# Two modulation blocks out of the first FFN1 step and into token mixing, one more moved inside the first FFN2 step

## The reference

```
cond = silu(c)
for l in range(2):
    mod = cond @ w_ada[l] + b_ada[l]              # 1024 x 9216
    sh1, sc1, g1, sh2, sc2, g2, sh3, sc3, g3 = split(mod, 9)
    h = rms_norm(x, norm_ffn1[l]) * (1 + sc1) + sh1
    x = x + 0.5 * g1 * swiglu(h, w_gate1[l], w_up1[l], w_down1[l])   # hidden 2816: FFN1
    h = rms_norm(x, norm_mix[l]) * (1 + sc2) + sh2
    x = x + g2 * token_mixing(h, w_in[l], ..., w_out[l])             # three kinds of attention, 16 heads
    h = rms_norm(x, norm_ffn2[l]) * (1 + sc3) + sh3
    x = x + 0.5 * g3 * swiglu(h, w_gate2[l], w_up2[l], w_down2[l])   # FFN2
```

## Time and profile before

| | |
|---|---|
| median of 3 timed runs | 1188.55 us (1175.79, 1188.55, 1189.0) |
| the profiled execution's own time | 1179.13 us |
| its span, first to last instruction | 1177.4 us |
| PE / PEld / DVE / ACT busy | 96% / 87% / 73% / 45% |
| mean granted clock of TensorE | 0.989 |
| HBM read | 256.56 MB, 219 GB/s over the span |

### The profile page before, as it was taken

One profiled execution on the slowest core, in us unless ns is written; L12 is line 12 of the kernel. 1 busy time (PEld: TensorE's weight loads), 2 busy tenths in 40 slices (PEclk: granted clock), 3 DMA queues, 4 the chain that ended last, 5 costly groups with the idle time before them and its releaser, 6 DMA issues.

```text
span 1177.4 us, 20277 instructions
## 1 busy us (share of the span) xinstructions
PE 1135.6 (96%) x7892; PEld 1024.1 (87%) x7892; DVE 864.5 (73%) x1263; ACT 530.3 (45%) x685; POOL 64.7 (5%) x79
## 2 busy tenths in 40 slices
PE   6899999999999999999998999999999998999998
PEld 3599999989898789999987999998989877999997
DVE  5787788798866877666777877888887588645545
ACT  3334334454566543433463344335456545433432
POOL 2101101100000000000001011000000000000000
PEclk9999999999999999999998999999999999999999
DMA  9898899945511667777747988995842155566451
GB/s 304 273 328 300 298 318 312 334 126 172 179 55 55 215 214 239 227 247 256 264 158 243 333 302 295 308 349 156 257 144 91 55 179 171 189 212 192 164 196 72
DMA packets 160371, 258.41 MB, mean 219 GB/s; under 512 B 8365, under 2 KB 127277, under 8 KB 160319
## 3 DMA queue, kind: packets, MB, share of 16 engines
q1 hardware_dynamic: 140739, 182.25, 46.8%
q0 software_dynamic: 19584, 75.50, 19.1%
HBM read 256.56 MB, written 1.05 MB: 219 GB/s over the span
## 4 chain that ended last, share of the span: by engine, by line
PE 81%; DVE 10%; ACT 3%; DVEq 2%; DMA 2%; issue 2%; SPq 0%; ACTq 0%
PE bank L1246 24%; PE bank L1247 24%; PE bank L1248 24%; DVE wlo L854 3%; DVE room L796 2%; PE bank L1585 2%; PE bank L1504 1%; DVEq L798 1%; ACT whi L458 1%; DMA xs<-in_x_dram 1%; DMA ada<-in_w_ada_dram 1%; PE bank L1489 1%; PE bank L1566 1%; DVE xn L955 1%; ACT hTf L486 1%
## 5 line engine op out<-in xcount | busy, mean ns | idle before, releaser
L1246 PE MATMUL bank<-hhi,whi 128*128 128x256 f32 (+1 forms) x1600 | 455.7, 285 | 0.0
L1248 PE MATMUL bank<-hhi,wlo 128*128 128x256 f32 (+1 forms) x1600 | 453.6, 283 | 0.0
L1247 PE MATMUL bank<-hlo,whi 128*128 128x256 f32 (+1 forms) x1600 | 453.5, 283 | 0.0
L458 ACT ACTIVATE whi<-raw 128x2048 fp32r<-128x2048 f32 (+1 forms) x174 | 321.6, 1851 | 8.7 <-PE bank L1693 5.3
L1246 PEld LDWEIGHTS bank<-hhi,whi 128*128 128x128 f32 (+1 forms) x1600 | 306.8, 192 | 4.0 <-issue 1.8
L1247 PEld LDWEIGHTS bank<-hlo,whi 128*128 128x128 f32 (+1 forms) x1600 | 306.8, 192 | 2.4 <-issue 0.5
L1248 PEld LDWEIGHTS bank<-hhi,wlo 128*128 128x128 f32 (+1 forms) x1600 | 306.7, 192 | 0.0
L854 DVE TENSOR_TENSOR wlo<-raw,whi 128x2048 fp32r<-128x2048 f32 (+2 forms) x130 | 281.7, 2196 | 20.0 <-ACT whi L458 19.4
L796 DVE SCALAR_TENSOR_TENSOR room<-ada,cT,room 128x512 f32 (+3 forms) x266 | 170.1, 639 | 22.0 <-issue 2.6
L510 ACT ACTIVATE eb<-bank 128x512 f32<-128x512 f32 x40 | 23.9, 597 | 343.7 <-PE bank L1248 343.7
L972 DVE TENSOR_TENSOR wlo<-raw,whi 128x1024 fp32r<-128x1024 f32 x44 | 53.9, 1225 | 139.7 <-ACT whi L458 138.7
(11 more groups left out here) (218 smaller groups left out, 1134.0 us busy)
## 6 DMA issues: line engine op xcount, KB each, us to landing
ada<-in_w_ada_dram POOLq DMA_DIRECT2D x68, 1024.0 KB, 6.0
raw<-in_w_gate_dram SPq DMA_DIRECT2D x44, 1024.0 KB, 5.9
raw<-in_w_up_dram SPq DMA_DIRECT2D x44, 1024.0 KB, 7.1
raw<-in_w_down_dram SPq DMA_DIRECT2D x44, 1024.0 KB, 6.1
raw<-in_w_in_dram SPq DMA_DIRECT2D x28, 1024.0 KB, 5.4
raw<-in_w_out_dram SPq DMA_DIRECT2D x8, 512.0 KB, 3.2
raw<-in_w_out_dram SPq DMA_DIRECT2D x4, 1024.0 KB, 5.9
room<-in_w_ada_dram POOLq DMA_DIRECT2D x3, 1024.0 KB, 14.0
```

The source lines that it names most:

```text
L458: last = act.activation(dst, src, ACT.Copy)
L1246: pe.matmul(ps, l_hi, r_hi, start=first, stop=False)
L1247: pe.matmul(ps, l_hi, r_lo, start=False, stop=False)
L1248: return pe.matmul(ps, l_lo, r_hi, start=False, stop=last)
```

## The change

Ten of the FFN1 steps (WF1) weigh two blocks each, and the first step none. Mixing weighs five (MID): two in the first projections as before, one ahead of `logits(l, "A0")`, one after `read_out(l, "C10")` and thus ahead of `logits(l, "A1")`, and one after the last slab of w_out. The first FFN2 step weighs its block from slot 1, between the `split_lo` of slot 0 and that of slot 1 for the next step, where it was at the step's start from slot 0. PE's twelve one-column sums between chunk 1 and chunk 2 of mixing become eight, each ahead of a group of three products of chunk 2 ("ki"); the four others go to the mixing tail, where they replace four matmuls of zeros. DVE's `split_lo` of the first FFN2 gate slab goes from between the two halves of the residual to ahead of the last `weigh_mid`; ACT's `split_hi` of the first FFN2 up slab goes from between the two halves of the boundary to ahead of them. At the start POOL waits for the second slab in slot 1 before its first load of the loop.

```diff
-    MID = ADA_L - 3 * NF
+    WF1 = NF - 1
+    MID = ADA_L - 2 * WF1 - NF
+    OWN = NF - AHEAD
...
+            pool.wait_ge(raw_full[1], 16)
             for l in range(L):
                 rows_l = l * KT
-                with pool.Fori(0, NF) as i:
+                with pool.Fori(0, WF1) as i:
                     for k in range(2):
                         fill(k, ada_turn(l, k, i + 1), bass.ds(rows_l, KT), bass.ds(i * (2 * CW) + (AHEAD + k) * CW, CW))
...
+                for n in range(OWN):
+                    m = ADA_L - OWN + n
+                    if n == 0:
+                        fill(1, ada_turn(l, 1, WF1 + 3), bass.ds(rows_l, KT), slice(m * CW, (m + 1) * CW))
+                    else:
+                        fill(0, ada_turn(l, 0, WF1 + 3 + n), bass.ds(rows_l, KT), slice(m * CW, (m + 1) * CW))
...
@@ ACT, boundary @@
-                    if n == 2 and t == 0:
-
-                        act.wait_ge(out_done, nth(l, len(OUT_CHUNKS) - 1, NSLOT + 2))
-                        split_hi(1, turn(l, U_FFN[1]))
@@ ACT, after the output product @@
-                act.wait_ge(out_done, nth(l, len(OUT_CHUNKS) - 1, NSLOT + 1))
-                split_hi(0, turn(l, U_FFN[1]))
+                for k in range(2):
+
+                    act.wait_ge(out_done, nth(l, len(OUT_CHUNKS) - 1, NSLOT + k + 1))
+                    split_hi(k, turn(l, U_FFN[1]))
...
@@ DVE, residual @@
-                    if n == 1 and t == 1:
-                        split_lo(0, turn(l, U_FFN[1]))
...
-            def ffn_step(l, which, i, ahead, after, weighs=True):
+            def ffn_step(l, which, i, ahead, after, weighs=True, first=False):
...
-                if which == 0:
-                    weigh_ada([i + ada_turn(l, k, 1) for k in range(2)], [0, 1],
-                              held[:, at_cols(i * (2 * CW), 2 * CW)].rearrange("p (a n) -> p a n", a=2))
-                elif weighs:
-                    weigh_ada([i + ada_turn(l, 0, NF + 2 + 1)], [0], held[:, at_cols(i * CW + CW, CW)].rearrange("p (a n) -> p a n", a=1))
+                if which == 0 and not first:
+                    weigh_ada([i + ada_turn(l, k, 0) for k in range(2)], [0, 1],
+                              held[:, at_cols(i * (2 * CW) - 2 * CW, 2 * CW)].rearrange("p (a n) -> p a n", a=2))
+                elif which == 1 and weighs and not first:
+                    weigh_ada([i + ada_turn(l, 0, WF1 + 3)], [0], held[:, at_cols(i * CW + CW, CW)].rearrange("p (a n) -> p a n", a=1))
...
                     split_lo(0, i + after)
+                    if which == 1 and first:
+                        weigh_ada([ada_turn(l, 1, WF1 + 3)], [1], held[:, CW:2 * CW].rearrange("p (a n) -> p a n", a=1))
                     split_lo(1, i + after)
...
@@ DVE, mixing @@
                     if n == 14:
+                        weigh_mid(l, 2)
                         logits(l, "A0")
                         minus_cum(l)
                         out_first(l, 0)
                         out_first(l, 1)
                         read_out(l, "C10")
+                        weigh_mid(l, 3)
                 logits(l, "A1")
...
+                read_modc(MODC_PRE + nth(l, MODC_L, 4), modc[:, off:off + 2 * CT], PS[3][:, 0:2 * CT]).then_inc(modc_read, 1)
                 y_gain(l, "C")
...
-                weigh_mid(l, 2)
+                split_lo(0, turn(l, U_FFN[1]))
+                weigh_mid(l, 4)
...
@@ PE, project, chunk "ki" @@
                         for k in range(KT):
+                            at_ = 4 * D + k * P
+                            one = pe.matmul(PS[6][:, k:k + 1], held[:, at_:at_ + P], ones[:, 0:1], start=True, stop=True)
                             last = three(bank[0:KW, 0:S], wh[:, k, 0:KW], wl[:, k, 0:KW], hhi[:, k, :], hlo[:, k, :], k == 0, k == KT - 1)
+                        one.then_inc(modc_done, 1)
...
                         pe.wait_ge(gate_read, nth(l, NB, 2))
-                        sum_held(nth(l, ACC_L, ACC_PRE + NF), 4 * D, 12, PS[6])
+                        pe.wait_ge(acc_ready, nth(l, ACC_L, ACC_PRE + WF1))
...
                 turn_probs(l, "A1", 0, 1)
-                keep_running(PS[3], 4)
+                sum_ada(nth(l, ACC_L, ACC_PRE + WF1 + 4), [0, 1], PS[3]).then_inc(modc_done, 1)
                 values(l, "A1")
                 turn_y(l, "C")
+                pe.wait_ge(modc_read, nth(l, 2, 2))
```

More of the change, by code:

```diff
@@ L68, in build @@
     AHEAD = 2 * D // CW
-    MID = ADA_L - 3 * NF
+    WF1 = NF - 1
+    MID = ADA_L - 2 * WF1 - NF
+    OWN = NF - AHEAD
     CT = CW // P
-    assert MID == 3 and KT * N_MOD == ADA_L * CT
+    assert MID == 5 and KT * N_MOD == ADA_L * CT
     ADA_PRE = 0
-    ADA_TURNS = (NF + 2 + NF, NF + 1)
+    ADA_TURNS = (WF1 + 3 + NF - 1, WF1 + 2 + 1)
     wide = lambda w: w.rearrange("l (k p) n -> p (l k) n", p=P)
@@ L322, in build @@
         MODC_PRE = 1
-        MODC_L = 4
+        MODC_L = 5
         ACC_PRE = len(WEIGHED)
-        ACC_L = NF + MID + NF
+        ACC_L = WF1 + MID + NF
         NB = 3
@@ L831, in weigh_mid @@
             def weigh_mid(l, m):
-                sums = acc[:, m:m + 1, :] if m < 2 else held[:, 0:CW].rearrange("p (a n) -> p a n", a=1)
-                weigh_ada([ada_turn(l, m % 2, NF + m // 2 + 1)], [m % 2], sums)
+                sums = acc[:, m % 2:m % 2 + 1, :] if m < 4 else held[:, 0:CW].rearrange("p (a n) -> p a n", a=1)
+                weigh_ada([ada_turn(l, m % 2, WF1 + m // 2 + 1)], [m % 2], sums)
             def read_modc(done, dst, bank):
@@ L988, in ffn @@
                 last_ada = which == 1 and l + 1 == L
-                with dve.Fori(0, MID if last_ada else NF - 1) as i:
+                ffn_step(l, which, 0, True, turn(l, U_FFN[which] + 1), first=True)
+                with dve.Fori(1, OWN if last_ada else NF - 1) as i:
                     ffn_step(l, which, i, True, turn(l, U_FFN[which] + 1))
                 if last_ada:
-                    with dve.Fori(MID, NF - 1) as i:
+                    with dve.Fori(OWN, NF - 1) as i:
                         ffn_step(l, which, i, True, turn(l, U_FFN[which] + 1), False)
```

21 lines of the change are left out of this document (10 added, 11 removed).

## The result

The changed kernel takes 1193.69 us (median of 4 runs, 1189.46 to 1197.79) and the kernel before, in its 4 runs, 1185.07 us: ratio 1.0094, 95% interval 1.0051 to 1.0137. It is 0.9% slower, inside 2% but clear of the measurement's noise, where I had forecast 3.6 us of gain. The profiled execution took 1191.8 us (span 1189.9, mean granted clock 0.973) against 1179.13 us (span 1177.4, clock 0.989) before: 12.5 us more span.

A forecast was written before the change was run, and what follows sets the result against it. PE, busy 1135.6 of 1177.4 us, bounds the kernel, so only its idle or lower-clock time can be won. -17.7 + 0 + 1.6 + 7.5 + 4.0 + 1.0 = -3.6 us against the 1188.55 us median: 1185.0 us, range 1166 to 1192.

The forecast's parts named there:

- First steps: First down product of each FFN, both layers: waits for gulo and their loss of clock go, 17.7 us gained.
- Front of mixing: Ahead of mixing's transposes: spread sums gain 0; PE idles 3.7 us in layer 0, clock loss behind it 1.6 us.
- the commonest of the four: Clock losses behind the waits at the FFNs' first down products: 1.63, 1.64, 2.14 and 1.52 us; 1.6 was taken.
- End of mixing: Weighing ahead of A1's logits: 7.5 us lost to delay and 4.0 us to clock, over both layers.
- rows 2 and 3: Profile rows of PE's four first-down-product waits for gulo, 2.98, 2.14, 4.28 and 2.16 us, each with loss of clock behind.
- the column sums that I named as the danger: End of mixing: sums replacing four matmuls of zeros, the kind of work behind which layer 0's clock fell.
- Boundary: Ahead of FFN2: DVE's split, now first, waits for ACT's high part in layer 1; 1.0 us later, bounds 0 and 2.6.
- B: Rival: no loss of clock at the new idle times, -9.2 us, 1179.4 us; chance 0.18.
- A: Rival: the end of mixing takes the block for nothing, -15.1 us, 1173.5 us; chance 0.12.
- C: Rival: clock lost again in the output product and at layer 1's boundary, +2.4 us, 1191.0 us; chance 0.20.

The follow-up runs named there:

- e4: Kernel before, with only the first FFN2 step's weighing moved behind the split of slot 0, still fed from slot 0: 1188.06 us, ratio 1.0058.
- e3: Changed kernel plus zeros (16 matmuls in layer 0, 3 in layer 1) ahead of the wait before mixing's third-chunk transposes: 1191.29 us, ratio 1.0081.
- e2: Changed kernel plus 14 matmuls of zeros ahead of the values of B1, in the place of PE's wait: 1181.31 us, ratio 0.9989.
- e6: e1 with the eight column sums in one block ahead of chunk "ki" again: 1170.86 us, ratio 0.9909.
- e7: e1 with the two moved splits ahead of FFN2 put back in their old places: 1170.47 us, ratio 0.9913.
- e10: Changed kernel, unchanged, profiled a second time: 1189.74 us.
- e9: Kernel before, unchanged, profiled a second time: 1179.03 us.
- e11: e8 plus two matmuls of zeros behind the 4th, 8th and 12th column sums at FFN1's end and layer 0's FFN2 end: 1171.24 us, ratio 0.9923.
- e1: Changed kernel with the weighing of the fourth mixing block moved ahead of DVE's read of C10: 1174.19 us, ratio 0.9934.
- e8: e5 with the splits ahead of FFN2 in their old places, as in e7: 1167.45 us, ratio 0.9873.
- e5: e1 plus the zeros of e3 ahead of the third chunk's transposes: 1172.54 us, ratio 0.9915.

## Why the prediction was wrong

**First steps: right, the closeness in part luck.** -17.4 us against -17.7 forecast; the second pair of profiles gives -13.6, since the kernel before lost less in its first step there (1.67 us of wait, no clock) and the start of each layer scatters. The waits at the four first down products are gone, the products are back at 5.6 us, and the new wait at FFN2's second one is 0.24 and 0.23 us where I had 0.4 (the terms of that working add up to 0.5). e4 adds what the working passed over lightly: the slot had to change too, or the gain turns into a wait of 4.57 us one step later.

**Front of mixing: the wait right, its price somewhat low.** I had the wait (4.13 us, forecast 3.7) and its releaser. For the clock behind it I took "1.6, the commonest of the four", bounds "0 and 2.2", and in layer 1 "I take 0". Measured behind the waits in the first pair of profiles: 3.8 and 1.9 us, of which e3 takes back 3.8 and 1.5, so this is clock, not the sums. Neither size is firm: over all profiles the zeros take 2.1 us off layer 0, and in layer 1 e2, e6, e7 and e10, with no zeros there, have 31.23 to 31.25 us, which is what e3 has with them. The 1.6 was low by about a quarter against that 2.1. Ahead of the waits stand 1.3 and 1.0 us more that I didn't have (35.6 to 37.0 us in layer 0 and 31.8 to 34.0 in layer 1 over the kernels with the new front, against 34.64 and 31.53). In layer 0 this is the short loss of clock near 240 us and not DVE's order: the kernels with the old front take 35.78 (e9) and 35.74 us (e4) too where they have that loss. In layer 1 no profile with the old front has such a loss and all with the new front but e11's do; why stays open.

**End of mixing: the delay right, the clock three times too small.** The step that failed is this one: the price of the clock behind the wait ahead of `values` of B1, "I price this between 0 and 2.7 us in each layer ... and take 2.0". Everything up to it held: the delay with the boundary is 9.3 us by e2, against 7.5 + 1.0 in the sum; A1's logits came 3.5 us later (forecast 3.7), PE's wait was 3.15 us (forecast 3.1), the clock fell. By e2 the clock cost 12.1 us in both layers, 6.0 in each, over twice the upper bound.

The bound came from places where PE goes back to dense work: behind an idle time in an FFN the product takes 1.5 to 2.4 us more (rows 2 and 3, e4), and the clock is back. Here 64- and 128-column matmuls, transposes and column sums follow, with ACT and DVE between them, and the clock stayed down for nearly all of 374 to 392 us. I carried a price from one kind of surroundings into another, and the column sums that I named as the danger were only four sums, eight of the 78 matmul records in the three windows. The length of the idle time doesn't set the price: 4.28 us of it in FFN1 of layer 1 cost 2.14 us, 3.15 us here cost 6.0. Nor does thin work bring the loss about by itself: in e1 the same work, begun at full clock, keeps it. That it is the thin work behind the wait that holds the clock down is argued from these rows; no run put other work behind the same wait.

By the trace, PE was busy in 17.32 of those 18 us (6.00 + 7.00 + 4.32), and the clock was low all the same. The Trainium skill, "TensorE: Matmul & The Clock Gate", tells in Part 1 (under "HAM oscillation") of a kernel with thin products whose clock was low for 53.3 of its 211 us, and puts that down to PE's wait for a transfer ahead of every group of matmuls. This stretch agrees in that a wait comes before the low clock; it differs in that one wait stands ahead of it and PE is busy in nearly all of the rest. The same part puts the cost of the ramp at less than 1% of a typical kernel's span. Here two such places reach that by themselves: 12.1 us, 1.0% of the span.

**Boundary: a small term, right in size.** Forecast 1.0 us, bounds 0 and 2.6. e7 against e1 gives 0.5 and 0.2 us, e8 against e5 1.1 and 0.1, and e1 shows the wait of ACT for its slab (1.18 us) in layer 0, where I had put it in layer 1.

**The rivals.** B (clock spared) fell: at the end of mixing, the clock was lost in both layers of both profiles of the changed kernel. But the argument against it, that all four waits of rows 2 and 3 had the loss, holds for that profile alone: in e9 one of the four, of 1.67 us, had none. A (the block costs nothing) fell by the logits of A1. C came nearest to the mechanism. It named the clock, lost in the thin end of mixing and gone in what follows, but as one more loss of 2.2 us a layer, which gave 1191.0 us; 1193.69 lies past even that. Its place was also not the one I gave: of the 12.1 us of clock 9.9 lie between A1's logits and the first output matmul, and only 2.2 in the output product and behind it.

**The sum, remade.** -17.4 (FFNs) + 8.0 (front) + 0.5 (middle) + 21.45 (end and boundary) = +12.5 us of span. Against the forecast of -3.6 that is 16.1 us off, of which 6.4 lie in the front and 9.0 at the end; in the second pair of profiles, +10.5, it is 14.1 us off, with 1.7 in the front, 7.8 at the end and 4.1 in the FFNs. So the end of mixing is the miss that stays. Against the median of four runs of the kernel before the change is only +8.6 us, since that median is 6 us above its profiled execution. The forecast of 1185.0 us started from 1188.55, some 8 us above the medians of the later runs of that kernel; that it lies only 8.7 us below 1193.69 is luck in that respect.

## What to carry to other kernels

A block of work that is moved off one wait is free only where its engine already waits for the bottleneck: ahead of DVE's read of C10 it cost 0.24 us, one line further down some 10 us a layer. Price an idle time of PE by what PE does behind it, as far as these few places go: 1.5 to 2.4 us where dense 512-column products followed, 6 us where thin ones did; where such an idle time can't be moved away, zeros of its length (3.2 us of them) bought the clock back whole. And where the block is fed through a slot, moving its use moves the next load of that slot too.

## What was unexpected of the hardware

After an idle time of some 3.15 us, PE stayed at 1.2 GHz over some 17 to 20 us in which it was nearly always busy with thin work, in both layers and in three profiles (the changed kernel's two and e3); eight 128x128 transposes took 1.91 us there and four column sums (eight records) 1.71 us, where in e1, at full clock, they took 1.04 and 0.95 us:

```profile
373.08 1.04 PE L1580 MATMUL bank<-ident,eb 128*128 128x128 f32 x8
373.97 0.95 PE L1266 MATMUL bank<-ones,acc 128*128 128x1 f32 x8
```

The same thin work, begun at full clock, kept it in e1. And the clock didn't fall in the idle time: its mean of 0.55 over 374 to 380 us puts the fall at about 374.6, some 0.7 us after PE had begun again at 373.93. Behind 4.13 us of idle time at the front of mixing, with 256-column products following from 274.5 us on, these matmuls go from 0.41 to 0.28 us each at 279 us. Short losses of some 3 us, by contrast, came and went at other places between two runs of one program (at 239 us in one of two), and zeros set among the sums next to them didn't remove them.
